# The value stage of the expert mixer: straight code, a third set of weight buffers, a third PSUM tile, weighing in quarters

## The chip, the cores and the metric

The kernel runs on one core of a Trainium2 chip. The metric is the device time of one execution in microseconds (us). Five engines work side by side: PE (TensorE, matmuls), DVE (VectorE), ACT (ScalarE), POOL (GpSimd) and SP, which only starts DMA transfers here. Each follows its own list of instructions in order; semaphores tie the lists together.

## What is computed

One inference step of a decoder layer for 512 prompt tokens and 8 sample tokens, 520 columns of width 2048, in float32: attention and a state-space layer side by side, an output projection, and then an expert mixer (PEER). The change lies in the last part of the mixer and in nothing else. The mixer picks 16 of 16384 experts per head and token:

```python
idx = jnp.take_along_axis(cand_i, top_p, axis=-1)
gate = jax.nn.softmax(top_s, axis=-1)
u = u_tab[idx]
act = jax.nn.gelu(jnp.einsum('thkd,td->thk', u, hb).astype(jnp.float32))
v = v_tab[idx].astype(jnp.float32)
return jnp.einsum('thk,thkd->td', gate * act, v).astype(h.dtype)
```

After it come the residual addition and a final norm.

## The kernel before

The 520 columns are split by how the experts are applied. For 360 of them (`ND`) the kernel computes all experts densely: the stage before (`stage_e`) multiplies the token matrix with all of `u_tab` and stores the activations and the gates in DRAM (`expert_acts`, `expert_gates`); the value stage, `stage_f`, multiplies gate x activation with all of `v_tab`. For the other 160 columns it fetches the chosen rows with indirect DMAs and sums them up: 128 steps of one row of 2048 numbers for each of 128 tokens (`vg`, 1 MB a step), and 128 steps of a quarter row for the other 32 tokens (`vgx`, 0.25 MB).

**Units.** `v_tab` comes as 128 units of 1 MB (`units`), a unit being 16 weight tiles of 128x128. A matmul in float32 is made of three matmuls on parts: weights and activations are each split into a rounded high part (`wh`, `vh`) and a rest (`wl`, `vl`), and `wh*vh + wh*vl + wl*vh` is summed in PSUM (lines 1940 to 1942). So a unit takes 2 output tiles (`VT`) x 8 expert blocks (`GRP`) x 3 = 48 matmuls of 360 columns. Eight units (`UPG`) make a group, which works on one set of 8 activation blocks; there are 16 groups (`NG`).

**The way of a unit.** SP asks for it (`load_unit`, line 116) when POOL has finished the low part of the unit two before it, whose raw buffer it takes. ACT casts the high part in two instructions (`split_hi`, line 122) once the raw data are there and PE has finished the unit two before (`tile_done`), whose buffers `wh` and `wl` it takes. POOL subtracts the low part in four instructions of 128x512 (`split_lo`, line 129); PE then multiplies. There are two sets of `raw`, `wh`, `wl`, by the parity of the unit.

**What else is in the lists.** POOL issues behind the low part of a unit 9/8 gathers of each kind on average (lines 1872 and 1877). DVE adds each finished output tile from PSUM to `x` (line 2025, 128x360), behind a unit's first tile it adds gathered rows (line 1984), behind its second the quarter rows (line 1991). PE may begin a tile when DVE has added the tile two before it (`sum_added`); there is one PSUM bank for each of a unit's two tiles. For the next group DVE multiplies activations by gates (`weigh`, line 1970), ACT casts the result to `vh` (`w_hi`, line 1885), DVE subtracts `vl` (`low`, line 1974), each in two halves of 128x1440, at the unit numbers 3, 4 and 5 of a group. SP's list also has the loads of the next activations (line 1839, 1.44 MB, behind unit request 1 of a group, when PE has begun the group) and gates (line 1843, 1.44 MB, behind unit request 5).

**Loops.** PE, ACT and SP run two groups per turn of a hardware loop, seven turns, and the last two groups as straight code. POOL and DVE have straight code throughout. The order in each list is the order of the code; no scheduler changes it.

The three lines that follow set when PE may start a unit and a tile:

```python
pe.wait_ge(m.lo_done, u + 3)
for d in range(VT):
    pe.wait_ge(S["sum_added"], i * (2 * UPG * VT) + (UPG * VT * gg + VT * n + d + 1))
```

Of the kernel before, what the change touches and what calls it, by code (L numbers as in the profile page):

```python
# [8 lines left out]
F32 = mybir.dt.float32  # L9
F32R = mybir.dt.float32r  # L10
# [5 lines left out]
ds = bass.ds  # L16
# [1314 lines left out]
UPG, VT = 8, 2  # L1331
GW = 4
# [461 lines left out]
def rows_by(j):  # L1794
    return min(HK, j * 9 // 8)
# [4 lines left out]
def rows_x_by(j):  # L1800
    return min(HK, max(0, (j - 1) * 9 // 8))

def stage_f(nc, m, ins, outs):
# [6 lines left out]
    y_sb = at("y_sb", [P, D]); yx_sb = at("yx_sb", [P, DX])  # L1810
    sq = at("sq3", [P, 4, T]); rs = at("rs3", [P, T])
    vgx = [at(f"vgx{j}", [P, DX]) for j in range(GX)]
# [5 lines left out]
    S = {n: sem("g_" + n) for n in "ain1 weighed weighed_hi weighed_lo sum_added tile_done rows_added y_kept y_turned squares_ready squares_added squares_summed root_ready out_ready out_stored x_added x_turned".split()}  # L1818
# [3 lines left out]
    halves = [slice(GRP // 2 * h, GRP // 2 * (h + 1)) for h in range(2)]  # L1822
    with nc.Block() as block:
        def turn_loads(sp, i, last):
            for gg in range(2):
                g = i * 2 + gg
# [327 lines left out]
```

## Time and profile before

| | |
|---|---|
| median of 3 runs | 3609.88 us (3597.08 to 3615.14) |
| profiled execution, its own time | 3603.36 us |
| its span | 3601.5 us |
| PE busy | 3347.8 us, 93% |
| POOL busy | 2335.4 us, 65% |
| DVE busy | 2195.3 us, 61% |
| ACT busy | 1105.8 us, 31% |
| DMA | 970.60 MB, mean 269 GB/s |

The profile is of one execution. Busy time counts the instructions of an engine; PE's matmuls overlap, so that each shows twice the time from one start to the next. "Idle before" an instruction is put down to what released it last. "Issue" is idle time in which an engine waited for nothing that the profile shows. The granted clock of PE is given as a share of 2.4 GHz. Times within the program are counted from the start of the span.

### The profile page before, as it was taken

What the parts mean: (1) busy time and instruction counts of PE and PEld (TensorE: products, weight loads), DVE (VectorE), ACT (ScalarE), POOL (GpSimd) and SP (SyncE); (2) the same over time, 40 slices, a digit from 0 to 9 for tenths busy, and PEclk for the clock granted to TensorE, in tenths of its full rate; (3) what the DMA queues carried; (4) which work ended last, traced back from release to release, by engine and by line L of the source; (5) the groups of instructions that cost most, each with busy time, mean ns of one, the idle gap of its engine ahead of it and who ended that gap; (6) DMA issues with size and microseconds to landing.
All of it is one profiled execution on the core that took longest, in us unless ns stands there. A gap on an engine that the chain in (4) does not pass through costs nothing. (4 is left out here: it accounts for less than half of the span.)

```text
span 3601.5 us, 58870 instructions
## 1 busy us (share of the span) xinstructions
PE 3347.8 (93%) x22639; PEld 3154.7 (88%) x22639; DVE 2195.3 (61%) x3999; ACT 1105.8 (31%) x1501; POOL 2335.4 (65%) x1923
## 2 busy tenths in 40 slices
PE   7999987889999999999999999988899899998997
PEld 7988853548998998999999999988898899898987
DVE  7832223335226999996887666444667566666654
ACT  4111132243223233444444344322222222222222
POOL 2533306003442458888888888877888888888874
PEclk9999988999999999999999999999999999999998
DMA  4597978672322235888888889878888888888863
GB/s 163 190 370 308 339 282 274 228 250 106 127 97 95 82 116 209 322 344 331 334 333 343 340 325 350 340 268 322 322 320 326 333 319 316 329 313 323 325 250 118
DMA packets 251675, 970.60 MB, mean 269 GB/s; under 512 B 44674, under 2 KB 108803, under 8 KB 172931
## 3 DMA queue, kind: packets, MB, share of 16 engines
q1 hardware_dynamic: 151394, 553.25, 42.6%
q0 software_dynamic: 57344, 335.58, 23.1%
q10 hardware_dynamic: 42720, 78.87, 6.0%
q8 instruction: 137, 2.24, 0.3%
q14 instruction: 80, 0.65, 0.0%
HBM read 891.32 MB, written 73.92 MB: 268 GB/s over the span
## 5 line engine op out<-in xcount | busy, mean ns | idle before, releaser
L129 POOL TENSOR_TENSOR wl<-raw,wh 128x512 fp32r<-128x512 f32 x1280 | 1712.6, 1371 | 791.7 <-ACT wh L122 789.3
L122 ACT ACTIVATE wh<-raw 128x1024 fp32r<-128x1024 f32 x648 | 650.6, 1052 | 2038.7 <-PE acc L1942 658.5
L1940 PE MATMUL acc<-vh,wh 128*128 128x360 f32 x2048 | 687.9, 336 | 107.1 <-DVE xt L2025 35.6
L1560 PE MATMUL acc<-hh,wh 128*128 128x360 f32 x2048 | 677.7, 331 | 8.0 <-POOL wl L129 8.0
L1942 PE MATMUL acc<-vh,wl 128*128 128x360 f32 x2048 | 683.0, 333 | 0.0
L1941 PE MATMUL acc<-vl,wh 128*128 128x360 f32 x2048 | 681.9, 333 | 0.0
L1562 PE MATMUL acc<-hh,wl 128*128 128x360 f32 x2048 | 671.3, 328 | 0.0
L1561 PE MATMUL acc<-hl,wh 128*128 128x360 f32 x2048 | 671.0, 328 | 0.0
L147 PE MATMUL acc<-hh,wh 128*128 128x256 f32 (+1 forms) x1920 | 547.7, 285 | 7.8 <-DVE tt L427 5.1
L148 PE MATMUL acc<-hl,wh 128*128 128x256 f32 (+1 forms) x1920 | 544.6, 284 | 0.0
L149 PE MATMUL acc<-hh,wl 128*128 128x256 f32 (+1 forms) x1920 | 543.2, 283 | 0.0
L1940 PEld LDWEIGHTS acc<-vh,wh 128*128 128x128 f32 x2048 | 395.9, 193 | 108.2 <-issue 49.8
L1941 PEld LDWEIGHTS acc<-vl,wh 128*128 128x128 f32 x2048 | 395.9, 193 | 16.4 <-issue 16.4
L1722 DVE SCALAR_TENSOR_TENSOR ug<-ug,aux 128x2048 f32<-128x2048 f32 x128 | 291.7, 2282 | 189.2 <-DMA ug<-expert_u,idx 188.4
L1984 DVE SCALAR_TENSOR_TENSOR aux<-vg,w,aux 128x2048 f32<-128x2048 f32 x127 | 298.8, 2353 | 175.4 <-DMA vg<-expert_v,idx 174.4
L1942 PEld LDWEIGHTS acc<-vh,wl 128*128 128x128 f32 x2048 | 395.4, 193 | 0.0
L1560 PEld LDWEIGHTS acc<-hh,wh 128*128 128x128 f32 x2048 | 384.6, 188 | 10.5 <-issue 10.5
L147 PEld LDWEIGHTS acc<-hh,wh 128*128 128x128 f32 x1920 | 364.2, 190 | 24.1 <-issue 24.0
L1561 PEld LDWEIGHTS acc<-hl,wh 128*128 128x128 f32 x2048 | 385.2, 188 | 0.0
L1562 PEld LDWEIGHTS acc<-hh,wl 128*128 128x128 f32 x2048 | 385.0, 188 | 0.0
L148 PEld LDWEIGHTS acc<-hl,wh 128*128 128x128 f32 x1920 | 363.9, 190 | 0.1
L149 PEld LDWEIGHTS acc<-hh,wl 128*128 128x128 f32 x1920 | 363.6, 189 | 0.0
(361 smaller groups left out, 4163.1 us busy)
## 6 DMA issues: line engine op xcount, KB each, us to landing
raw<-units SPq DMA_DIRECT2D x324, 1024.0 KB, 4.9
kr<-cache_k SPq DMA_DIRECT2D x128, 512.0 KB, 6.6
vr<-cache_v SPq DMA_DIRECT2D x128, 512.0 KB, 6.0
expert_acts<-ast ACTq DMA_DIRECT2D x128, 180.0 KB
expert_gates<-gs ACTq DMA_DIRECT2D x15, 1536.0 KB, 7.2
a<-expert_acts SPq DMA_DIRECT2D x16, 1440.0 KB, 11.1
g<-expert_gates SPq DMA_DIRECT2D x16, 1440.0 KB, 10.9
output_steps<-qo ACTq DMA_DIRECT2D x16, 288.0 KB, 6.6
```

The source lines that it names most:

```text
L122: act.activation(m.wh[s][:, k:k + KT // 2, :], m.raw[s][:, k:k + KT // 2, :], ACT.Copy).then_inc(m.hi_done, 1)
L129: x = pool.tensor_tensor(m.wl[s][:, part, :], m.raw[s][:, part, :], m.wh[s][:, part, :].bitcast(F32), ALU.subtract)
L147: pe.matmul(o, m.wh[s][:, k, :], rhs_hi[:, k, c0:c0 + n], start=(k == k_range[0]), stop=False)
L148: pe.matmul(o, m.wh[s][:, k, :], rhs_lo[:, k, c0:c0 + n], start=False, stop=False)
L149: mm = pe.matmul(o, m.wl[s][:, k, :], rhs_hi[:, k, c0:c0 + n], start=False, stop=(k == k_range[-1]))
L1560: pe.matmul(o, m.wh[s][:, k, :], m.hh[:, k, N0:T], start=(k == 0), stop=False)
L1561: pe.matmul(o, m.wh[s][:, k, :], m.hl[:, k, N0:T], start=False, stop=False)
L1562: mm = pe.matmul(o, m.wl[s][:, k, :], m.hh[:, k, N0:T], start=False, stop=(k == KT - 1))
L1940: pe.matmul(o, m.wh[s][:, VT * e + d, :], vh[gg][:, e, :], start=(e == 0), stop=False)
L1941: pe.matmul(o, m.wh[s][:, VT * e + d, :], vl[gg][:, e, :], start=False, stop=False)
L1942: mm = pe.matmul(o, m.wl[s][:, VT * e + d, :], vh[gg][:, e, :], start=False, stop=(e == GRP - 1))
L1984: dve.scalar_tensor_tensor(y_tok, vg[k % GW][:, :], m.w0[:, k:k + 1], y_tok, ALU.mult, ALU.add).then_inc(S["rows_added"], 1)
```

## The change

- `stage_f` has no loops: PE, ACT and SP get straight code.
- `raw`, `wh`, `wl` come in three sets (`RW`); unit v uses set v mod 3. SP asks for unit v when the low part of unit v-3 is done, and ACT casts it when PE has finished unit v-3.
- Output tiles go to three PSUM banks in turn (`AW`), so that PE may begin a tile when the tile three before has been added.
- `weigh`, `w_hi` and `low` work on four quarters of 128x720 (`NQ`), `weigh` behind the second tile of units 2 to 5 of a group, `low` behind that of units 3 to 6.
- The gates are loaded behind unit request 1 of a group (2 in the first), the activations behind request 4. At the start the raw request of unit 2 goes ahead of the gates.
- POOL's gathers stand one unit later in its list. Scratch buffers move to make room.

```diff
@@ -1329,6 +1329,7 @@
 NEG = -3.0e38
 GRP, NG = 8, 16
 UPG, VT = 8, 2
+RW, AW, NQ = 3, 3, 4
 GW = 4
...
 def rows_by(j):
-    return min(HK, j * 9 // 8)
+    return min(HK, max(0, (j - 1) * 9 // 8))
...
 def rows_x_by(j):
-    return min(HK, max(0, (j - 1) * 9 // 8))
+    return min(HK, max(0, (j - 2) * 9 // 8))
...
     vh = [at(f"vh{s}", [P, GRP, ND], F32R) for s in range(2)]
-    y_sb = at("y_sb", [P, D]); yx_sb = at("yx_sb", [P, DX])
...
+    raw, wh, wl = (x + [at(n, [P, KT, P], dt)] for x, n, dt in ((m.raw, "raw2", F32), (m.wh, "wh2", F32R), (m.wl, "wl2", F32R)))
+    vgx = [at(f"vgx{j}", [P, DX]) for j in range(GX - 1)]
     assert m.end <= m.x0 + 3 * KT * T * 4
...
+    vgx.append(at(f"vgx{GX - 1}", [P, DX]))
+    sq = at("sq3", [P, 4, T], off=m.first_off); rs = at("rs3", [P, T], off=m.first_off + 4 * T * 4)
+    y_sb = at("y_sb", [P, D], off=m.first_off + GRP * ND * 4); yx_sb = at("yx_sb", [P, DX], off=m.first_off + GRP * ND * 4 + D * 4)
+    tile_acc = (m.acc[:, 0, 0, 0:ND], m.acc[:, 0, 1, 0:ND], m.acc[:, 1, 1, 0:ND])
...
+    raw_in = m.raw_in + [S["raw2_in"]]
...
+    parts = [slice(GRP // NQ * q, GRP // NQ * (q + 1)) for q in range(NQ)]
...
-        def turn_loads(sp, i, last):
...
-                    if end and n >= UPG - 2:
-                        continue
-                    load_unit(m, sp, i * (2 * UPG) + (U_EXP_V + UPG * gg + n + 2), n % 2)
-                    if n == 1 and not end:
-                        load_acts(sp, g, 1 - gg)
-                    if n == 5 and not end and not (last and gg == 0):
-                        load_gates(sp, g)
-
-        def load_acts(sp, g, s):
-            sp.wait_ge(S["tile_done"], g * (UPG * VT) + 1)
-            sp.dma_start(a4[s][:, :, :], m.aD[ds(g * GRP + GRP, GRP), :, :].rearrange("e p n -> p e n")).then_inc(ain[s], 16)
-
-        def load_gates(sp, g):
-            sp.wait_ge(S["weighed"], g * GRP + 2 * GRP)
-            sp.dma_start(m.gates[:, :, :, :].rearrange("p b e n -> p b (e n)"), m.gD[:, :, ds(g * GRP + 2 * GRP, GRP), :].rearrange("b p e n -> p b (e n)")).then_inc(m.gates_in, 16)
...
-            sp.wait_ge(S["weighed"], GRP)
-            sp.dma_start(m.gates[:, :, :, :].rearrange("p b e n -> p b (e n)"), m.gD[:, :, GRP:2 * GRP, :].rearrange("b p e n -> p b (e n)")).then_inc(m.gates_in, 16)
-            with sp.Fori(0, NG // 2 - 1) as i:
-                turn_loads(sp, i, False)
-            turn_loads(sp, NG // 2 - 1, True)
+            for v in range(2, N_EXP):
+                if v >= RW:
+                    sp.wait_ge(m.lo_done, U_EXP_V + v)
+                sp.dma_start(raw[v % RW][:, :, :].rearrange("p k n -> p (k n)"), m.units[U_EXP_V + v, :, :]).then_inc(raw_in[v % RW], 16)
+                g, n = v // UPG, v % UPG
+                if n == (2 if g == 0 else 1) and g + 1 < NG:
+                    sp.wait_ge(S["weighed"], GRP * g + GRP)
+                    sp.dma_start(m.gates[:, :, :, :].rearrange("p b e n -> p b (e n)"), m.gD[:, :, GRP * g + GRP:GRP * g + 2 * GRP, :].rearrange("b p e n -> p b (e n)")).then_inc(m.gates_in, 16)
+                if n == 4 and g + 1 < NG:
+                    if g > 0:
+                        sp.wait_ge(S["tile_done"], UPG * VT * g)
+                    sp.dma_start(a4[(g + 1) % 2][:, :, :], m.aD[GRP * g + GRP:GRP * g + 2 * GRP, :, :].rearrange("e p n -> p e n")).then_inc(ain[(g + 1) % 2], 16)
...
-                u = U_EXP_V + j
                 if j < N_EXP - 2:
-                    split_lo(m, pool, u + 2, u % 2)
+                    v = j + 2
+                    for k in range(0, KT, KT // 4):
+                        if k % (KT // 2) == 0:
+                            pool.wait_ge(m.hi_done, (U_EXP_V + v) * 2 + (1 + 2 * k // KT))
+                        part = slice(k, k + KT // 4)
+                        x = pool.tensor_tensor(wl[v % RW][:, part, :], raw[v % RW][:, part, :], wh[v % RW][:, part, :].bitcast(F32), ALU.subtract)
+                    x.then_inc(m.lo_done, 1)
...
-            def w_hi(g, s, h):
-                act.wait_ge(S["weighed"], g * GRP + (GRP + GRP // 2 * (h + 1)))
-                act.wait_ge(S["tile_done"], g * (UPG * VT) + 1)
-                act.activation(vh[s][:, halves[h], :], a4[s][:, halves[h], :], ACT.Copy).then_inc(S["weighed_hi"], GRP // 2)
+            def w_hi(g, q):
+                act.wait_ge(S["weighed"], GRP * g + GRP // NQ * (q + 1))
+                if g >= 2:
+                    act.wait_ge(S["tile_done"], UPG * VT * (g - 1))
+                act.activation(vh[g % 2][:, parts[q], :], a4[g % 2][:, parts[q], :], ACT.Copy).then_inc(S["weighed_hi"], GRP // NQ)
...
-                for gg in range(2):
-                    end = last and gg == 1
-                    for n in range(UPG):
-                        if not (end and n >= UPG - 2):
-                            split_hi(m, act, i * (2 * UPG) + (U_EXP_V + UPG * gg + n + 2), n % 2, i * UPG + ((U_EXP_V + UPG * gg) // 2 + n // 2 + 1),
-                                     (S["tile_done"], i * (2 * UPG * VT) + (UPG * VT * gg + VT * (n + 1))))
-                        if n in (3, 4) and not end:
-                            w_hi(i * 2 + gg, 1 - gg, n - 3)
...
-            with act.Fori(0, NG // 2 - 1) as i:
-                turn(i, False)
-            turn(NG // 2 - 1, True)
-            for k in range(KT - 2, KT):
+            for v in range(2, N_EXP):
+                act.wait_ge(raw_in[v % RW], raw_count(v))
+                if v >= RW:
+                    act.wait_ge(S["tile_done"], VT * (v - RW + 1))
+                for k in range(0, KT, KT // 2):
+                    act.activation(wh[v % RW][:, k:k + KT // 2, :], raw[v % RW][:, k:k + KT // 2, :], ACT.Copy).then_inc(m.hi_done, 1)
+                g, n = (v - 2) // UPG, (v - 2) % UPG
+                if 3 <= n < 3 + NQ and g + 1 < NG:
+                    w_hi(g + 1, n - 3)
+                if v == N_EXP - UPG:
+                    act.wait_ge(S["rows_added"], HK)
+                    act.wait_ge(S["x_added"], HK)
+                    for g in range(4):
+                        act.activation(y_sb[:, 512 * g:512 * g + 512], m.aux[:, g, :], ACT.Copy)
+                    act.activation(yx_sb[:, :], yx, ACT.Copy).then_inc(S["y_kept"], 1)
+                if v - RW >= N_EXP - UPG:
+                    for k in range(VT * (v - RW - N_EXP + UPG), VT * (v - RW - N_EXP + UPG + 1)):
...
         def _(pe):
-            def turn(i, last):
-                for gg in range(2):
-                    for n in range(UPG):
-                        u = i * (2 * UPG) + (U_EXP_V + UPG * gg + n)
-                        s = n % 2
-                        pe.wait_ge(m.lo_done, u + 3)
-                        for d in range(VT):
-                            pe.wait_ge(S["sum_added"], i * (2 * UPG * VT) + (UPG * VT * gg + VT * n + d + 1))
-                            o = m.acc[:, 0, d, 0:ND]
-                            for e in range(GRP):
-                                if n == 0 and d == 0:
-                                    pe.wait_ge(S["weighed_lo"], i * (2 * GRP) + (GRP * gg + e + 1))
-                                pe.matmul(o, m.wh[s][:, VT * e + d, :], vh[gg][:, e, :], start=(e == 0), stop=False)
-                                pe.matmul(o, m.wh[s][:, VT * e + d, :], vl[gg][:, e, :], start=False, stop=False)
-                                mm = pe.matmul(o, m.wl[s][:, VT * e + d, :], vh[gg][:, e, :], start=False, stop=(e == GRP - 1))
-                            mm.then_inc(S["tile_done"], 1)
...
-            with pe.Fori(0, NG // 2 - 1) as i:
-                turn(i, False)
-            turn(NG // 2 - 1, True)
+            for v in range(N_EXP):
+                g, n, b = v // UPG, v % UPG, v % RW
+                pe.wait_ge(m.lo_done, U_EXP_V + v + 3)
+                for d in range(VT):
+                    r = VT * v + d
+                    pe.wait_ge(S["sum_added"], r + 1)
+                    for e in range(GRP):
+                        if n == 0 and d == 0:
+                            pe.wait_ge(S["weighed_lo"], GRP * g + e + 1)
+                        pe.matmul(tile_acc[r % AW], wh[b][:, VT * e + d, :], vh[g % 2][:, e, :], start=(e == 0), stop=False)
+                        pe.matmul(tile_acc[r % AW], wh[b][:, VT * e + d, :], vl[g % 2][:, e, :], start=False, stop=False)
+                        mm = pe.matmul(tile_acc[r % AW], wl[b][:, VT * e + d, :], vh[g % 2][:, e, :], start=False, stop=(e == GRP - 1))
+                    mm.then_inc(S["tile_done"], 1)
...
-            dve.sem_inc(S["sum_added"], VT)
-            def weigh(g, h):
-                s = g % 2
-                dve.wait_ge(ain[s], (g // 2) * 16 + 16)
+            dve.sem_inc(S["sum_added"], AW)
+            def weigh(g, q):
+                dve.wait_ge(ain[g % 2], (g // 2) * 16 + 16)
                 dve.wait_ge(m.gates_in, g * 16 + 16)
-                a = a4[s][:, halves[h], :].rearrange("p e (b n) -> p e b n", b=NB)
-                dve.tensor_tensor(a, a, m.gates[:, :, halves[h], :].rearrange("p b e n -> p e b n"), ALU.mult).then_inc(S["weighed"], GRP // 2)
-            def low(g, h):
-                s = g % 2
-                dve.wait_ge(S["weighed_hi"], g * GRP + GRP // 2 * (h + 1))
-                dve.tensor_tensor(vl[s][:, halves[h], :], a4[s][:, halves[h], :], vh[s][:, halves[h], :].bitcast(F32), ALU.subtract).then_inc(S["weighed_lo"], GRP // 2)
+                a = a4[g % 2][:, parts[q], :].rearrange("p e (b n) -> p e b n", b=NB)
+                dve.tensor_tensor(a, a, m.gates[:, :, parts[q], :].rearrange("p b e n -> p e b n"), ALU.mult).then_inc(S["weighed"], GRP // NQ)
+            def low(g, q):
+                dve.wait_ge(S["weighed_hi"], GRP * g + GRP // NQ * (q + 1))
+                dve.tensor_tensor(vl[g % 2][:, parts[q], :], a4[g % 2][:, parts[q], :], vh[g % 2][:, parts[q], :].bitcast(F32), ALU.subtract).then_inc(S["weighed_lo"], GRP // NQ)
...
-                        dve.tensor_tensor(x, x, m.acc[:, 1, 1, :].rearrange("p (c q n) -> p q c n", c=4, n=NX), ALU.add)
+                        dve.tensor_tensor(x, x, m.acc[:, 1, 0, :].rearrange("p (c q n) -> p q c n", c=4, n=NX), ALU.add)
...
-                        dve.tensor_tensor(x, x, m.acc[:, 0, d, 0:ND], ALU.add).then_inc(S["sum_added"], 1)
+                        dve.tensor_tensor(x, x, tile_acc[r % AW], ALU.add).then_inc(S["sum_added"], 1)
...
-                        if d == 0 and g + 1 < NG and n in (3, 4):
-                            weigh(g + 1, n - 3)
-                        if d == 1 and g + 1 < NG and n in (4, 5):
-                            low(g + 1, n - 4)
+                        if d == 1 and g + 1 < NG and 2 <= n < 2 + NQ:
+                            weigh(g + 1, n - 2)
+                        if d == 1 and g + 1 < NG and 3 <= n < 3 + NQ:
+                            low(g + 1, n - 3)
```

Two places in the lists show it. The first is SP's queue in the loop (before) and in a later group (now); `raw_61`, `raw_62` and `raw_21629` are the raw buffers, `a` the activations and `g` the gates. Before, one half of the loop's body:

```order
L116 DMA raw_62<-units 128x2048
L1838 ISA
L1839 ISA
L1839 DMA a_21624<-expert_acts 128x8x360
L115 REGISTER_ALU
L116 ISA
L116 DMA raw_61<-units 128x2048
```

Now, from the gates to the activations of one group:

```order
L1848 DMA g_13571<-expert_gates 128x15x192
L1844 DMA raw_21629<-units 128x2048
L1844 DMA raw_61<-units 128x2048
L1844 DMA raw_62<-units 128x2048
L1852 DMA a_13570<-expert_acts 128x8x360
```

The register work is gone, the raw requests go round three buffers, and gates and activations have traded places within the group.

The second is DVE in the units in which the next group is weighed; `xt<-xt,acc` is the addition of a tile, `aux` and the second `acc` are the sums of gathered rows. Before:

```order
L2025 TENSOR_TENSOR xt<-xt,acc 128x360
L1991 SCALAR_TENSOR_TENSOR acc<-vgx_21636,wx,acc 128x512
L1974 TENSOR_TENSOR vl_21626<-a_21624,vh_21628 128x1440
L2025 TENSOR_TENSOR xt<-xt,acc 128x360
L1984 SCALAR_TENSOR_TENSOR aux<-vg_21638,w_13556,aux 128x2048
```

Now:

```order
L1980 SCALAR_TENSOR_TENSOR acc<-vgx_21632,wx,acc 128x512
L1960 TENSOR_TENSOR a_21624<-a_21624,g_13571 128x720
L1963 TENSOR_TENSOR vl_21626<-a_21624,vh_21628 128x720
L2014 TENSOR_TENSOR xt<-xt,acc 128x360
L1973 SCALAR_TENSOR_TENSOR aux<-vg_21637,w_13556,aux 128x2048
```

A piece of weighing and a piece of low part, half as long each, now stand together behind the second tile.

## Rows read from the trace of the kernel before

**Rows 1.** Stretches: value stage, stage before, 80 units; column heads first

```profile
core 0: us, PE busy (x) PEld busy (x) DVE busy (x) ACT busy (x) POOL busy (x), PEclk, DMA share, GB/s
2423.30:3577.40 1154.10, 1059.64 (x6163) 1042.39 (x6164) 719.58 (x601) 307.90 (x308) 941.13 (x760) 0.96 0.80 303
1296.80:2410.00 1113.20, 1103.60 (x6894) 1100.44 (x6893) 846.23 (x1543) 443.50 (x493) 944.87 (x768) 1.00 0.83 314
2578.36:3298.43 720.07, 661.74 (x3840) 650.37 (x3841) 473.74 (x380) 188.22 (x180) 613.70 (x500) 0.96 0.85 322
```

**Rows 2.** Timeline of PE: start us, us, engine, line, instruction [idle before <-releaser]

```profile
2822.68 0.32 PE L1940 MATMUL acc<-vh,wh 128*128 128x360 f32 x1
...
2824.00 0.32 PE L1942 MATMUL acc<-vh,wl 128*128 128x360 f32 x1
2827.39 0.43 PE L1940 MATMUL acc<-vh,wh 128*128 128x360 f32 x1 [3.07 <-POOL wl L129]
...
2829.47 0.50 PE L1941 MATMUL acc<-vl,wh 128*128 128x360 f32 x1
```

**Rows 3.** Waits of PE, value stage: us in total, times, longest

```profile
PE acc L1940 <- DVE xt L2025: 35.6, 32, 3.9
PE acc L1940 <- POOL wl L129: 31.7, 12, 10.8
PE acc L1940 <- issue: 26.7, 11, 3.0
PE acc L1940 <- DVE vl L1977: 12.7, 1, 12.7
```

**Rows 4.** Timeline of PE at a back edge of the loop

```profile
2864.75 0.43 PE L1940 MATMUL acc<-vh,wh 128*128 128x360 f32 x1 [2.27 <-issue]
...
2870.05 0.46 PE L1940 MATMUL acc<-vh,wh 128*128 128x360 f32 x1 [2.56 <-issue]
```

**Rows 5.** Groups by line, PE, 3305 to 3577.4 us, behind the last back edge

```profile
L1940 PE MATMUL acc<-vh,wh 128*128 128x360 f32 x507 | 168.8, 333 | 13.1 <-DVE xt L2025 8.6 <-POOL wl L129 4.5
```

**Rows 6.** Groups by line, POOL, the 80 units: busy us, mean ns | idle before

```profile
L129 POOL TENSOR_TENSOR wl<-raw,wh 128x512 fp32r<-128x512 f32 x320 | 417.2, 1337 | 63.6 <-ACT wh L122 62.8
L1872 POOL DMA_INDIRECT vg<-expert_v,idx x90 | 104.5, 1162 | 15.3 <-issue 12.5
L1877 POOL DMA_INDIRECT vgx<-expert_v,idxx x90 | 92.9, 1032 | 27.4 <-issue 27.4
```

**Rows 7.** Timeline of POOL and of DVE, unit 14

```profile
2560.34 5.03 POOL L129 TENSOR_TENSOR wl<-raw,wh 128x512 fp32r<-128x512 f32 x4
2565.52 2.19 POOL L1872 DMA_INDIRECT vg<-expert_v,idx  x1 [0.16 <-issue]
2568.02 0.95 POOL L1877 DMA_INDIRECT vgx<-expert_v,idxx  x1 [0.30 <-issue]
...
2561.04 5.85 DVE L1974 TENSOR_TENSOR vl<-a,vh 128x1440 fp32r<-128x1440 f32 x1
```

**Rows 8.** Timeline of SP's queue and of ACT, start of the value stage

```profile
2428.96 10.15 SPq L116 DMA_DIRECT2D raw<-units  x2
...
2446.70 2.00 ACT L122 ACTIVATE wh<-raw 128x1024 fp32r<-128x1024 f32 x2 [18.00 <-DMA raw<-units]
2449.18 2.00 ACT L122 ACTIVATE wh<-raw 128x1024 fp32r<-128x1024 f32 x2 [0.48 <-DMA raw<-units]
```

**Rows 9.** DMA: all of 2578 to 3298 us; the fastest 8 us (columns as Rows 1)

```profile
DMA packets 61453, 231.84 MB, mean 322 GB/s; under 512 B 4480, under 2 KB 33920, under 8 KB 39680
...
2812.00:2820.00 8.00, 7.79 (x47) 7.79 (x48) 4.98 (x7) 0.00 (x0) 5.55 (x5) 1.00 1.03 414
```

**Rows 10.** Timeline of PE, the larger part of the transposes of y

```profile
3512.89 1.91 PE L1950 MATMUL aux<-ident,y_sb 128*128 128x128 f32 x16
```

**Rows 11.** Groups by line, DVE, the 80 units

```profile
L1984 DVE SCALAR_TENSOR_TENSOR aux<-vg,w,aux 128x2048 f32<-128x2048 f32 x90 | 211.7, 2353 | 117.8 <-DMA vg<-expert_v,idx 116.9
L2025 DVE TENSOR_TENSOR xt<-xt,acc 128x360 f32<-128x360 f32 x160 | 83.7, 523 | 128.3 <-PE acc L1942 128.3
L1991 DVE SCALAR_TENSOR_TENSOR acc<-vgx,wx,acc 128x512 f32<-128x512 f32 x90 | 67.3, 748 | 1.0
```

More of the change, by code:

```diff
@@ L1809, in stage_f @@
     vh = [at(f"vh{s}", [P, GRP, ND], F32R) for s in range(2)]
-    y_sb = at("y_sb", [P, D]); yx_sb = at("yx_sb", [P, DX])
-    sq = at("sq3", [P, 4, T]); rs = at("rs3", [P, T])
-    vgx = [at(f"vgx{j}", [P, DX]) for j in range(GX)]
+    raw, wh, wl = (x + [at(n, [P, KT, P], dt)] for x, n, dt in ((m.raw, "raw2", F32), (m.wh, "wh2", F32R), (m.wl, "wl2", F32R)))
+    vgx = [at(f"vgx{j}", [P, DX]) for j in range(GX - 1)]
     assert m.end <= m.x0 + 3 * KT * T * 4
@@ L1821, in stage_f, with raw_count @@
     vgx_in = [sem(f"g_vgxin{j}") for j in range(GX)]
[L1822 removed]
+    parts = [slice(GRP // NQ * q, GRP // NQ * (q + 1)) for q in range(NQ)]
+    def raw_count(v):
+        return 16 * ((U_EXP_V // 2 + 1 if v % RW < 2 else 1) + v // RW)
     with nc.Block() as block:
[L1824 to L1843 removed]
         def load_tiles(eng, n):
@@ L1895, in square @@
                     act.wait_ge(S["squares_added"], k - 3)
-                act.wait_ge(S["sum_added"], VT + UPG * VT * (NG - 1) + k + 1)
+                act.wait_ge(S["sum_added"], AW + UPG * VT * (NG - 1) + k + 1)
                 act.activation(sq[:, k % 4, :], m.xt[:, k, :], ACT.Square).then_inc(S["squares_ready"], 1)
-            def turn(i, last):
-                for gg in range(2):
-                    end = last and gg == 1
-                    for n in range(UPG):
-                        if not (end and n >= UPG - 2):
-                            split_hi(m, act, i * (2 * UPG) + (U_EXP_V + UPG * gg + n + 2), n % 2, i * UPG + ((U_EXP_V + UPG * gg) // 2 + n // 2 + 1),
-                                     (S["tile_done"], i * (2 * UPG * VT) + (UPG * VT * gg + VT * (n + 1))))
-                        if n in (3, 4) and not end:
-                            w_hi(i * 2 + gg, 1 - gg, n - 3)
-                        if last and gg == 0 and n == UPG - 2:
-                            act.wait_ge(S["rows_added"], HK)
-                            for g in range(4):
-                                act.activation(y_sb[:, 512 * g:512 * g + 512], m.aux[:, g, :], ACT.Copy)
-                            act.wait_ge(S["x_added"], HK)
-                            act.activation(yx_sb[:, :], yx, ACT.Copy).then_inc(S["y_kept"], 1)
-                        if end and n >= 1:
-                            for k in range(VT * n - 2, VT * n):
-                                square(k)
@@ L1921, in _ @@
+            for k in range(VT * (UPG - RW), KT):
                 square(k)
@@ L1954, in _ @@
-            with pe.Fori(0, NG // 2 - 1) as i:
-                turn(i, False)
-            turn(NG // 2 - 1, True)
+            for v in range(N_EXP):
[11 more added lines that the diff above has]
+                    mm.then_inc(S["tile_done"], 1)
+                if v == N_EXP - UPG - 1:
+                    pe.wait_ge(S["y_kept"], 1)
+                    for c in range(4):
+                        mm = pe.transpose(m.acc[:, 1, 0, P * c:P * c + P], yx_sb[:, P * c:P * c + P], m.ident[:, :])
+                    mm.then_inc(S["x_turned"], 1)
+                    for k in range(KT):
+                        mm = pe.transpose(m.aux[:, k // 4, P * (k % 4):P * (k % 4) + P], y_sb[:, P * k:P * k + P], m.ident[:, :])
+                        if k % 4 == 3:
+                            mm.then_inc(S["y_turned"], 1)
```

15 lines of the change are left out of this document (2 added, 13 removed).

## The prediction

> **What bounds the kernel now.** I read the stretch view first. The value stage runs from 2423.3 to 3577.4 us, 1154.1 us, with PE busy 92% and its clock at 0.96. The stage before it, with as many weight units and some 730 small matmuls more, keeps PE busy 99% at clock 1.00 in 1113.2 us [rows 1]. So the value stage loses what its twin doesn't. The floor: eight starts between 2822.68 and 2824.00 are 0.165 us apart [rows 2]; a unit has 48 matmuls, 7.91 us, and 128 units take 1012.5 us. The stage is 141.6 us above that. The waits of PE name 35.6 us for DVE's tile additions, 31.7 us for POOL's low parts, 26.7 us as "issue", and 12.7 us at the first low activations [rows 3]: 106.7 us. The other 35 us are the clock: after an idle time of 3.07 us the matmuls soon show 0.50 us instead of 0.33 [rows 2], the 1.2 GHz level instead of 2.4; it lasts for 12 of them, whose starts are 0.30 us apart. Clock loss follows long idle times, and goes when they go.
>
> "Issue" has a place. It is where the loop of 16 units branches back: PE stops 2.27 us there and 2.56 us eleven matmuls later [rows 4], at each of the six back edges. After the last back edge, over 32 units of which the last 16 are straight code, PE never waits on issue [rows 5].
>
> The other two waits come from an engine that PE hardly shows. POOL per unit, over 80 units in the loop (720.07 us, 9.00 us each): 417.2 + 104.5 + 92.9 us busy, and 12.5 + 27.4 us of issue gaps between its DMA requests [rows 6]. That is 654.5 us, **8.18 us a unit, more than PE's 7.91**. POOL is idle only 62.8 us [rows 6], because with two sets of buffers it can't begin a unit's low part before PE has left the set: it may never work ahead, and it never makes up for a late raw unit.
>
> **The change, part by part.**
>
> *Loops out on PE, SP, ACT.* Removed: six back edges, each 4.8 us idle and some 12 slow matmuls of 0.135 us extra, 6.5 us, so 39 us. They aren't a gain of their own: behind them POOL is late next, so they count only down to POOL's pace, below. Added: 5376 matmuls of code to fetch. Straight code showed no issue wait in rows 5, so zero; the ends are zero and one stop of 2.27 us plus slow clock at any interval (a rival).
>
> *Three sets of weight buffers.* A raw unit was asked for when the low part two units earlier ended, now three earlier. POOL needs it 2 x 9.00 - 5.03 - 1.05 = 11.9 us later before, and about 3 x 8.35 - 6.1 = 19 us later now (5.03 us is one burst of four low-part subtractions [rows 7], 1.05 us a half of the cast, 2.00 us [rows 8]). The slowest landing took from 2428.96 to 2446.70, 17.7 us [rows 8]. So a late raw unit is covered, and cast and low part of a unit can start a unit earlier. POOL can now work without idling: this is the part that pays. SP's queue: the gates request now waits for the last quarter of weighing and holds back the raw requests behind it by a few us; the 19 us cover it. If that cover were gone, the raw unit would be late as before, about 3 us of PE every two groups [rows 2].
>
> *Tiles in three PSUM banks.* DVE may be one tile (3.95 us) later before PE waits. That hides most of the 35.6 us. What is late next is POOL.
>
> *Weighing in quarters.* DVE's low part of 1440 elements, begun at 2561.04 inside a burst of POOL's, took 5.85 us and ended 1.5 us after the burst [rows 7]: 1.5 us is its work, the rest a wait for the memory port that both use. In turn POOL's request at 2565.52 took 2.19 us instead of 0.95, while DVE held the port. Free of each other, POOL needs 5.03 + 1.125 x 2 x 0.95 + 39.9/80 = 7.67 us a unit (1.125 is 90 requests of each kind on 80 units). Eight pieces of 720 elements, 0.85 us each (on the line from 0.52 us for 360 elements [rows 11] to 1.5 us for 1440), are 6.8 us a group, 0.85 a unit, and a POOL that never idles can lose all of it. Bounds of POOL's need: 8.18 (as measured, with idle time in which to hide) and 7.67 + 0.85 = 8.52. I take 8.35, between the two, because POOL's idle share, which hid part of it, goes.
>
> The Trainium skill (SBUF — State Buffer, the section on the shared port pair) says that the loser of that port blocks until the winner's instruction ends. Rows 7 differ: DVE waited past the ends of all four of POOL's subtractions. By the page DVE would wait 1.26 us at most, its tiles would never be late, and POOL would lose the port at every piece: 8.52 us a unit, and the sum would be 19 us higher.
>
> *Gathers one unit later in POOL's list.* POOL itself is a unit earlier, so they go out at the same time in PE's terms. Nothing.
>
> *The start.* Raw unit 2 was asked for at 2428.96, behind gates and x tiles, and cast at 2446.70, with PE idle 10.8 us [rows 3, 8]. Now it goes first, about 2422, and units 3 and 4 take its old places: casts at 2446.7 and 2449.2. PE wants unit 3 at 2449.7 and gets it at 2453: 3 us. Unit 5 comes behind the 1.44 MB of activations, 2.5 MB more at some 375 GB/s, an estimate from the loop's 322 GB/s on average and 414 GB/s in the fastest 8 us [rows 9], 6.6 us: POOL starts its low part at 2457 and from there has no reason to idle.
>
> *The sum.* Low part of unit 115, the last one before which gathers stand, ends at 2457 + 110 x 8.35 + 5.03 = 3380.5. Then 13 units of PE, 102.8 us, and the transposes, 2 us [rows 10], and 1 us of waits: PE ends at 3486 instead of 3577.4. Saved: 91.5 us. The end of the program behind it (norm and stores) is as before. The profiled execution took 3603.4 us, so 3512; the median of the runs is 6.5 us above it, so **3518 us** as a median, 2.5% less.
>
> **Rivals.**
>
> *PE becomes the bound* (POOL loses nothing to the port and keeps 7.67). For it: in the stage before PE was 99% busy with the same POOL work. Against: there a unit took 8.7 us because of the extra matmuls. Then PE ends at 2423.3 + 1012.5 + 1.6 (one spell of slow clock) + 3 + 2 = 3442.4, 135 us saved: 3475.
>
> *DVE holds the tiles back: slower.* Product and low part now stand together behind the second tile of five units in eight. DVE's unit: 2 x 0.52 + 1.125 x (2.35 + 0.75) + 2 x 0.85 = 6.2 us [rows 11], and 11.3 us if it waits out one burst of 5.03 us each time, 16.3 if POOL takes the port between the two. PE runs ahead of it by only three tiles. At 11.3 us for five units it falls 14.8 us behind the 8.35, and with the one tile of 3.95 us that it may be later PE would stop 11 us a group, 165 us over 15 groups: 3683. It decides from 91/75 = 1.2 us a unit on. For it: PE does wait for DVE's additions now [rows 3]. Against: having waited for a burst's end, DVE is next back one POOL period later, in the same gap of POOL's, so it is as slow as POOL and no slower. A mild form, a quarter to a third of that, gives 3560 to 3573.
>
> *DMA is the bound.* The loop moved 231.84 MB in 720 us, 2.90 MB a unit, at a busy share of 0.85 [rows 1, 9]; 8.35 us a unit asks for 347 GB/s and a share of 0.92. For it: 0.92 leaves little room. Against: 414 GB/s was reached for 8 us, at a share of 1.03 [rows 9], and this is 19% above what is asked for. If 322 GB/s were the ceiling, the loop would stay at 9.0 us a unit and only start and end gain: 3590, no change.
>
> *Code fetch stalls straight code: slower.* 2.3 to 3 us idle and the slow clock, some 4.6 us a stop; from 20 stops, one in 6 units, it eats the gain. Against: rows 5.
>
> **How the numbers follow.** POOL's pace 0.70 (3490 to 3550), PE's 0.10 (3475), DVE in its mild form 0.08, in its strong one 0.04, DMA 0.05, code fetch 0.03 (half of it slower). A run of this kernel tells 0.5%, 18 us, from no change. Faster by more: 0.70 + 0.10 + 0.08 + a third of the DMA case, 0.90; within: 0.04; slower: 0.06. The range, 3474 to 3562, takes in PE's pace below, POOL at 8.52 us (3537) and the beginning of the mild DVE case above.
>
> **What would show it.** No issue waits on PE in the value stage; ACT's casts waiting for raw data only at the start; POOL idle by under 2% between 2457 and the last gather, with 8.2 to 8.6 us a unit; clock 0.99; PE's remaining waits under 1 us each, on the low parts or on tile additions. Wrong if POOL still waits for casts and PE for DVE's additions by over 1 us in the weighing units (DVE), if raw landings of over 19 us appear (DMA), or if "issue" is back (code).

## The result and the profile after

Four runs of the changed kernel gave a median of **3572.66 us** (3566.12 to 3575.93); the kernel before, beside it, 3607.48 us (4 runs). The ratio is 0.9893, 95% interval 0.9867 to 0.9918: faster by 1.1%. The forecast was 3518 us, 2.5% less, with a range from 3474 to 3562. The direction was right; the size was not, and the time lies outside the range. The profiled execution took 3571.98 us, its span is 3570.2 us.

Windows of the changed kernel; the columns are those of [rows 1], and the first stretch is the value stage:

```profile
2419.40:3547.30 1127.90, 1048.89 (x6164) 1043.42 (x6164) 790.31 (x666) 312.20 (x340) 923.93 (x760) 0.96 0.81 310
```

The stage takes 1127.9 us and ends at 3547.3, where 3486 was forecast. The clock is still 0.96, so long stops of PE are still there. The waits of PE in this stage, to be held against [rows 3]:

```profile
PE acc L1935 <- DVE xt L2014: 69.4, 14, 6.4
PE acc L1935 <- DVE vl L1966: 12.8, 1, 12.8
PE acc L1935 <- POOL wl L1867: 7.0, 2, 5.6
```

The issue waits are gone, and POOL's 31.7 us have become 7.0. But the wait for the tile additions has doubled, from 35.6 to 69.4 us, and the number of times fell from 32 to 14: fewer and longer stops, each followed by slow matmuls. They come once a group, and from the second group on at the same place, before the fourth of its eight units. The other engines' waits in the stage:

```profile
ACT wh L1905 <- DMA raw<-units: 274.5, 40, 13.2
DVE aux L1973 <- DMA vg<-expert_v,idx: 245.8, 64, 9.6
...
POOL wl L1867 <- ACT wh L1905: 128.7, 32, 15.1
```

So POOL isn't the engine that never idles, as was forecast: it waits for ACT's casts for 128.7 us. Raw data come late, and so do gathered rows. One group of the timeline shows how the three belong together. SP's queue first, then POOL, ACT, DVE and PE (columns as in [rows 2]):

```profile
2857.59 32.96 SPq L1844 DMA_DIRECT2D raw<-units  x5
2906.81 0.38 SPq L1848 DMA_DIRECT2D g<-expert_gates  x1
2907.23 7.06 SPq L1844 DMA_DIRECT2D raw<-units  x3
2914.44 0.43 SPq L1852 DMA_DIRECT2D a<-expert_acts  x1
...
2893.06 5.03 POOL L1867 TENSOR_TENSOR wl<-raw,wh 128x512 fp32r<-128x512 f32 x4
2898.25 1.45 POOL L1872 DMA_INDIRECT vg<-expert_v,idx  x1 [0.16 <-issue]
...
2900.98 5.03 POOL L1867 TENSOR_TENSOR wl<-raw,wh 128x512 fp32r<-128x512 f32 x4
...
2914.09 1.45 POOL L1872 DMA_INDIRECT vg<-expert_v,idx  x1 [0.16 <-issue]
...
2922.62 5.05 POOL L1867 TENSOR_TENSOR wl<-raw,wh 128x512 fp32r<-128x512 f32 x4 [5.83 <-ACT wh L1905]
2927.81 0.96 POOL L1872 DMA_INDIRECT vg<-expert_v,idx  x1
...
2921.48 2.01 ACT L1905 ACTIVATE wh<-raw 128x1024 fp32r<-128x1024 f32 x2 [11.92 <-DMA raw<-units]
...
2903.41 3.37 DVE L1960 TENSOR_TENSOR a<-a,g 128x720 f32<-128x720 f32 x1
...
2937.71 4.81 DVE L1973 SCALAR_TENSOR_TENSOR aux<-vg,w,aux 128x2048 f32<-128x2048 f32 x2 [9.24 <-DMA vg<-expert_v,idx]
2942.44 0.52 DVE L2014 TENSOR_TENSOR xt<-xt,acc 128x360 f32<-128x360 f32 x1
...
2943.11 0.64 PE L1935 MATMUL acc<-vh,wh 128*128 128x360 f32 x1 [5.07 <-DVE xt L2014]
2943.54 0.50 PE L1936 MATMUL acc<-vl,wh 128*128 128x360 f32 x1
```

Read it from the top. POOL's low part ends at 2898.09 and frees a raw buffer, but SP stands at the gates request, which waits for the last product piece; that piece ends at 2906.78. The raw request goes at 2907.23, 9.1 us late, and ACT casts that unit from 2921.48 on, 23.4 us after its buffer came free. While SP stands there the DMA engines run dry, and then they get gates (1.44 MB), three raw units in 7 us and the activations (1.44 MB) at once. The hold is 9.1 or 9.2 us at all 14 gates requests behind the first. In the kernel before no raw request goes over 1 us after its buffer came free: there the gates are asked for behind unit 7 of a group, counted as in the change by the unit asked for, and weighing is over before the next buffer comes free. Windows of the same group:

```profile
2903.36:2908.36 5.00, 5.00 (x32) 5.00 (x32) 5.00 (x5) 1.50 (x2) 4.54 (x5) 1.00 0.23 75
2918.36:2923.36 5.00, 5.00 (x32) 5.00 (x32) 1.25 (x3) 1.88 (x2) 0.74 (x1) 1.00 1.02 424
2938.36:2943.36 5.00, 0.26 (x1) 0.29 (x2) 4.89 (x4) 1.78 (x2) 4.67 (x5) 0.82 1.03 424
```

The share falls to 0.23 and then is 1.00 or more for some 35 us. ACT waits 11.92 us for raw data and POOL 5.83 us for ACT. The gathers stand behind that low part in POOL's list, so the next one goes 13.7 us after the last one (2914.09 to 2927.81) instead of 7.9, and into full DMA engines. DVE waits 9.24 us for its row, with the tile additions behind it in its list, and PE runs out of its three tiles and stops for 5.07 us.

### The profile page after: what moved, and what is told of

The parts are those of the page before. It is cut to its first block and busy times, and to the rows that moved or that the text cites. A ratio compares the mean times of both kernels' runs of the same rounds, so it can differ in the third digit from the quotient of the medians.

```text
span 3570.2 us, 58151 instructions
## 1 busy us (share of the span) xinstructions
PE 3331.6 (93%) x22639; PEld 3149.4 (88%) x22639; DVE 2276.9 (64%) x4059; ACT 1109.2 (31%) x1531; POOL 2319.5 (65%) x1923
## 5 line engine op out<-in xcount | busy, mean ns | idle before, releaser
L1935 PE MATMUL acc<-vh,wh 128*128 128x360 f32 x2048 | 683.9, 334 | 89.4 <-DVE xt L2014 69.4
L1867 POOL TENSOR_TENSOR wl<-raw,wh 128x512 fp32r<-128x512 f32 x504 | 649.8, 1324 | 130.7 <-ACT wh L1905 128.7
L1562 PEld LDWEIGHTS acc<-hl,wh 128*128 128x128 f32 x2048 | 385.0, 188 | 0.0
L1563 PEld LDWEIGHTS acc<-hh,wl 128*128 128x128 f32 x2048 | 384.9, 188 | 0.0
## 6 DMA issues: line engine op xcount, KB each, us to landing
a<-expert_acts SPq DMA_DIRECT2D x16, 1440.0 KB, 18.4
g<-expert_gates SPq DMA_DIRECT2D x16, 1440.0 KB, 11.2
```

The costliest lines, as they stand in the source:

```text
L1562: pe.matmul(o, m.wh[s][:, k, :], m.hl[:, k, N0:T], start=False, stop=False)
L1563: mm = pe.matmul(o, m.wl[s][:, k, :], m.hh[:, k, N0:T], start=False, stop=(k == KT - 1))
L1867: x = pool.tensor_tensor(wl[v % RW][:, part, :], raw[v % RW][:, part, :], wh[v % RW][:, part, :].bitcast(F32), ALU.subtract)
L1935: pe.matmul(tile_acc[r % AW], wh[b][:, VT * e + d, :], vh[g % 2][:, e, :], start=(e == 0), stop=False)
```

## The experiments

All times are medians. The ratio is to the kernel before, run beside each on the same chip; "early" means gathers as in the kernel before. Edits are to the changed kernel unless another is named. e1 to e4 ran on one chip, e5 to e8 on a second, e9 to e11 on a third and e12 on a fourth, and the kernel before took 3610.8, 3621.0, 3612.8 and 3617.8 us beside them. Between these sets the ratios are to be compared; a difference of times can be off by some 10 us.

| run | us | ratio, 95% interval |
|---|---|---|
| e1, gates request later | 3494.18 | 0.9668 [0.9638, 0.9697] |
| e2, gathers early | 3484.73 | 0.9648 [0.9621, 0.9675] |
| e3, small gates request | 3506.34 | 0.9708 [0.9679, 0.9738] |
| e4, before, loops written out | 3599.57 | 0.9965 [0.9945, 0.9985] |
| e5, e1 and e2 | 3506.72 | 0.9680 [0.9659, 0.9701] |
| e6, before, gathers late | 3969.21 | 1.0964 [1.0940, 1.0989] |
| e7, e2, two sets of weight buffers | 3532.25 | 0.9752 [0.9733, 0.9770] |
| e8, e2, two tile banks | 3490.25 | 0.9649 [0.9630, 0.9667] |
| e9, e2, weighing in halves | 3512.25 | 0.9721 [0.9701, 0.9742] |
| e10, e2, two banks and halves | 3514.03 | 0.9721 [0.9701, 0.9742] |
| e11, e2, first gates request later | 3487.60 | 0.9658 [0.9637, 0.9680] |
| e12, e10 with two sets of weight buffers | 3562.28 | 0.9843 [0.9792, 0.9894] |

### The chain through SP's list and POOL's list

**e1: the gates request two raw requests later in a group.**

```diff
-                if n == (2 if g == 0 else 1) and g + 1 < NG:
+                if n == (2 if g == 0 else 3) and g + 1 < NG:
```

> The changed kernel, with the gates request behind raw request 3 of a group instead of 1. Theory Q (SP's queue): the gates request waits for the last quarter of weighing and holds two raw requests back by about 8 us; then gates, three raw units and activations are on the queue at once, POOL is starved of raw data, the gathers behind its low part come late, and DVE waits for a gathered row ahead of its tile additions, which stops PE 5 us once a group. With the request moved, SP does not wait; the stop shrinks below 2 us and 15 groups give back 4 to 7 us each: 3470 to 3515. Theory D (DMA is at its ceiling whatever the order): within 5 us of 3570. Theory P (the port pieces of DVE): unchanged as well, with the stops where they are.

**e2: the gathers back where they were in POOL's list.**

```diff
 def rows_by(j):
-    return min(HK, max(0, (j - 1) * 9 // 8))
+    return min(HK, j * 9 // 8)
 def rows_x_by(j):
-    return min(HK, max(0, (j - 2) * 9 // 8))
+    return min(HK, max(0, (j - 1) * 9 // 8))
```

> The changed kernel, with the gathers in POOL's list where they stood before (one unit earlier). Theory Q: the raw data are as late as in the changed kernel and POOL waits as long, but the rows that DVE wants were requested ahead of the starved low part; the waits of DVE for rows (245.8 us) fall below 120 and PE's stops to under 2 us: 3480 to 3520. Theory D: the same bytes arrive in the same time, 3565 to 3575. Theory P: no change.

Either edit alone is enough: 78 us less than the changed kernel for e1, 88 us for e2. In e1 the gathers are as late in POOL's list as in the change, but no raw request behind the gates is late any more. The waits of PE in e1:

```profile
PE acc L1935 <- DVE xt L2014: 16.9, 10, 3.6
```

and in e2, where the tile additions are late only once:

```profile
PE acc L1935 <- POOL wl L1867: 10.2, 13, 4.1
...
PE acc L1935 <- DVE xt L2014: 1.1, 1, 1.1
```

The expectation for e2 gave the time, but not the way. It had raw data as late as in the changed kernel, POOL waiting as long, and DVE's waits for rows below 120 us; these are 160.1 us, and POOL doesn't wait between 2500 and 3200 us. The same places of SP's and POOL's lists in e2:

```profile
2868.05 0.38 SPq L1848 DMA_DIRECT2D g<-expert_gates  x1
2868.47 14.95 SPq L1844 DMA_DIRECT2D raw<-units  x3
...
2862.20 5.05 POOL L1867 TENSOR_TENSOR wl<-raw,wh 128x512 fp32r<-128x512 f32 x4
```

The low part ends at 2867.25 and the raw request goes 1.2 us later, not 9.1, in each of the 14 groups. So e2 takes away the first link as well as the last. DVE can't go on before its gather, so a gather that stands behind one low part more makes POOL stand one unit further ahead of PE: from the end of a unit's low part to PE's start on it there are 8.2 us, median of units 8 to 119, in the changed kernel, and 0.6 us in e2; it is 6.8 us in e1, with late gathers, and 0.2 in e5, with early ones. The raw buffer comes free that much earlier, while the end of weighing, for which the gates request waits, stays where PE and DVE are. Most of the 9.1 us is thus the work of the shift of the gathers itself.

ACT waits 430.5 us for raw data in e2, more than in the changed kernel, and it costs nothing while POOL is kept busy. POOL's groups in e2, 2500 to 3200 us (columns as in [rows 6]), and the windows of a stretch:

```profile
L1867 POOL TENSOR_TENSOR wl<-raw,wh 128x512 fp32r<-128x512 f32 x349 | 439.6, 1295 | 1.6
L1872 POOL DMA_INDIRECT vg<-expert_v,idx x97 | 119.6, 1233 | 16.8 <-issue 16.8
L1877 POOL DMA_INDIRECT vgx<-expert_v,idxx x99 | 93.8, 948 | 30.2 <-issue 30.2
...
2873.00:3390.00 517.00, 510.98 (x3080) 506.01 (x3079) 418.76 (x333) 154.03 (x165) 480.38 (x399) 1.00 0.92 354
```

Here is the state that the prediction described: POOL doesn't idle (1.6 us before 349 subtractions), the clock is 1.00, and the chain of waits of the whole program lies 24% on POOL. 349 subtractions are 87.25 units, so a unit takes POOL 8.02 us.

**e5: both edits together.** Its diff is those of e1 and e2.

> The changed kernel with both edits, the gates request behind raw request 3 and the gathers one unit earlier in POOL's list. Theory Q says that the two are links of one chain (SP holds raw units back, POOL starves, the gathers behind its low part are late), so that breaking it once more gives no more: the early gathers alone left 13 us over PE's floor. 3476 to 3488. If they were two separate losses, 1.5 to 2% each, it would come to 3410, which PE's floor forbids; if the later gates request harms, 3490 or more.

No gain on top. By the time it is 22 us more than e2, on another chip; the ratios, 0.9680 and 0.9648, have intervals that overlap. PE's waits for low parts have grown:

```profile
PE acc L1935 <- POOL wl L1867: 24.0, 26, 4.1
```

The gates are now asked for shortly ahead of the activations, and the two land in 12.9 and 21.6 us, median, against 11.2 and 19.9 in e2. Whether two transfers so close together are what costs time wasn't tried apart. Since e2 alone has a hold of only 1.2 us left, e5 had no second link to cut. Read from the other side it says more: against e1, with the gates request in the same late place, it puts the gathers back and gains nothing (0.9680 and 0.9668). The late gathers cost nothing that can be told once the gates request is out of the way.

**e3: the gates request fetches 1 of its 15 blocks, from the third group on.** The weighing there multiplies by stale gates.

```diff
+                    nb = NB if g < 2 else 1
-                    sp.dma_start(m.gates[:, :, :, :]
+                    sp.dma_start(m.gates[:, 0:nb, :, :]
```

> The changed kernel; from the third group on the gates request fetches 1 of its 15 blocks (0.1 MB instead of 1.44 MB), so the weights by gates are computed from stale gates, and SP's order and waits stay. 1.35 MB less a group is 3.3 us of the 410 GB/s that the burst shows. Theory D: the group gets about 3 to 4 us shorter, 13 groups, 3520 to 3530. Theory Q: the burst is shorter by 3.3 us, so raw data and rows come 3 us earlier and the stop of 5.3 us and the slow matmuls behind it shrink by 3 to 5 us a group: 3505 to 3530. Theory P: no change. It tells P from the other two.

The hold of SP is there as before (the three raw requests behind the gates still go within 7.1 us), only 1.35 of the 1.44 MB of gates are gone, and 66 us with them. PE's waits for tile additions fall to 25.7 us in 13 stops:

```profile
PE acc L1936 <- DVE xt L2015: 25.7, 13, 7.2
```

The longest of them, 7.2 us, stands in a group whose gates are still whole. So the hold alone costs a small part. The long stop needs the burst of transfers behind it.

One figure goes with all of these runs: the longest time from a raw buffer's coming free to the landing of the unit that takes it, over units 16 to 119. It is 24.7 us in the changed kernel, 18.4 in e1, 15.9 in e2, 18.7 in e3 and 20.4 in e5. The prediction had said that 19 us are covered.

**e6: the kernel before, with its gathers one unit later.** The diff is that of e2 turned round, on the kernel before.

> The kernel before, with only the gathers moved one unit later in POOL's list. The prediction held this move to cost nothing because POOL is a unit earlier; in the kernel before POOL is not. A row would be asked for 9 us later than DVE's list wants it: from a unit's end 7.4 us to the request, 8.6 to land, 2.9 for the row and the tile behind it, 18.9 us, which two banks allow only 1.5 unit times: 12.6 us a unit instead of 9.0, 3900 to 4070. If DVE's wait for rows were harmless to PE: 3600 to 3650.

The step which the prediction had priced at nothing costs 348 us where there are two tile banks and two sets of buffers. POOL can't be a unit earlier there, so this isn't the case that the prediction spoke of; it is the price without that lead. The waits of PE and of DVE:

```profile
PE acc L1940 <- DVE xt L2025: 336.0, 53, 8.7
...
DVE aux L1984 <- DMA vg<-expert_v,idx: 714.5, 116, 11.0
```

DVE waits for 116 of the 128 rows, and PE for the tile additions behind them. A stop also lasts longer than the wait says, since slow matmuls follow it: the mean clock of this program is 0.935.

### The parts of the change one by one

**e4: the kernel before with the loops of the value stage written out, on SP, ACT and PE.**

```diff
-            with pe.Fori(0, NG // 2 - 1) as i:
+            for i in range(NG // 2 - 1):
```

> The kernel before, with nothing but its loops in the value stage written out (PE, ACT, SP). The six back edges cost 4.8 us idle and 1.6 us of slow clock each, 39 us. If PE's own stops bound the stage, 3565 to 3575. If POOL's pace does (8.18 us a unit against 9.0), part of it comes back as waits on POOL and DVE: 3575 to 3595. If straight code had a fetch cost: 3610 or more, with issue waits.

The waits of PE in e4:

```profile
PE acc L1940 <- DVE xt L2025: 67.6, 32, 5.1
PE acc L1940 <- POOL wl L129: 26.9, 16, 9.5
```

The 26.7 us of issue are gone. In their place the wait for tile additions has grown from 35.6 to 67.6 us: 0.35% is left, less than the expectation gave. It fits that DVE and POOL caught up while PE stood at a back edge; this was not tried apart.

**e7, e8, e9, e10, e11 and e12** all start from e2, so that the chain above doesn't hide what a part is worth:

```diff
-RW, AW, NQ = 3, 3, 4
+RW, AW, NQ = 2, 3, 4      (e7)
+RW, AW, NQ = 3, 2, 4      (e8)
+RW, AW, NQ = 3, 3, 2      (e9)
+RW, AW, NQ = 3, 2, 2      (e10)
+RW, AW, NQ = 2, 2, 2      (e12)
-                    sp.wait_ge(m.lo_done, U_EXP_V + v)
+                    sp.wait_ge(m.lo_done, U_EXP_V + v + 3 - RW)      (e7, e12)
-                if n == (2 if g == 0 else 1) and g + 1 < NG:
+                if n == (4 if g == 0 else 1) and g + 1 < NG:      (e11)
```

> The changed kernel with the early gathers (e2) and two sets of weight buffers instead of three, the rest as in the change. A raw unit then has 2 x 7.91 - 6.1 = 9.7 us to land; in the burst behind the gates it takes 13 to 18. If the third set is the part that pays: one stop of 4 to 8 us a group and slow matmuls behind it, 3560 to 3610. If straight code, banks and quarters carry the gain: 3485 to 3500.

> The changed kernel with the early gathers (e2) and tiles in two PSUM banks instead of three. DVE's tile addition may then be 3.95 us late instead of 7.9; behind a port wait of 3.4 us and a row it is about 4 to 6. If the third bank carries a part: waits on DVE of 1 to 2 us in the weighing units, 3510 to 3560. If it does nothing: 3480 to 3490.

> e2 (the changed kernel with early gathers) with weighing in halves of 128x1440 instead of quarters. In e2 POOL never idles between 2500 and 3200 us, at 8.0 us a unit, and each piece of weighing costs it 0.50 us at its next gather request. If quarters are worth something, halves make DVE hold the port 1.65 us at a time and its tile additions 5 to 8 us late: waits on DVE of 1 to 3 us twice a group, 3500 to 3540. If only the sum of port time counts, half as many pieces cost POOL as much or less: 3475 to 3488.

> e2 with two tile banks and weighing in halves: of the change only straight code, the third set of weight buffers and the order of SP's loads stand. If the third set is what lets POOL work without idling, and banks and quarters only soften DVE's lateness: 3490 to 3530, well below the 0.9965 of straight code alone. If banks and quarters carry the gain: 3560 to 3600.

> e2, with the first gates request behind the raw requests of units 3 and 4 instead of 2, so that those go out at once. It should take away the 4.1 us that PE waits for unit 3 at the start: 2 to 5 us less than e2, 3478 to 3484. If the gates of group 1 come too late for the first weighing: 3485 to 3495.

> The change with early gathers, but with two sets of weight buffers, two tile banks and weighing in halves: what is left is straight code and the new order in SP's list. Theory: the third set is most of the gain; on top of the plain order it is worth at least what it was on top of everything (48 us, e7 against e2), and more, because two banks and halves leave PE and POOL nothing to make up with: 3565 to 3600, and PE waits for POOL's low parts over 46 us. Rival A: straight code and the order of the requests carry the gain, and the third set is worth 48 us or less here too: 3535 to 3562. Rival B: without the third set nothing is left of the gain, as in e4 (3599.57): 3600 or more.

*Third set of weight buffers:* 1.0% (the ratios of e7 and e2) and 1.2% (e12 and e10, where e12's interval is half a per cent either way), less than expected of e7. On e7's own chip e8, which has three sets and two banks, is 42 us faster. In e12 a low part is late for 23.0 us in all, not for the 46 expected, and POOL waits 35.0 us for ACT within 700 us, where its idle time before subtractions is 1.6 us in e2 and in e10. PE waits another 44.1 us for tile additions there. The two gains agree within the intervals, so none is seen to depend on banks and quarters. *Third tile bank:* nothing in the time that can be told (the ratio of e8 is that of e2, and e10 is 1.8 us above e9). It does hide waits: with two banks and early gathers PE waits for DVE 17 times, but with POOL as the limit its waits for low parts fall from 10.2 to 3.7 us.

```profile
PE acc L1935 <- DVE xt L2014: 15.1, 17, 2.6
PE acc L1935 <- POOL wl L1867: 3.7, 1, 3.7
```

*Quarters:* 27.5 us (e9 against e2), 0.7% by the ratios. The time lies where the expectation put it, but not for its reason: PE waits for DVE once, 3.3 us. The cause shows in POOL's groups in e9, over the same 700 us as e2:

```profile
L1867 POOL TENSOR_TENSOR wl<-raw,wh 128x512 fp32r<-128x512 f32 x340 | 427.8, 1293 | 1.6
L1872 POOL DMA_INDIRECT vg<-expert_v,idx x96 | 130.2, 1356 | 16.8 <-issue 16.8
```

340 subtractions are 85 units, 8.24 us each against 8.02: the gather requests take 1356 ns instead of 1233 on average. Beside a piece of 1440 elements on DVE one takes 2.20 us, median of 41; beside one of 720 it takes 1.45 us, median of 69 in e2. Over 110 units that is 23 us. *The start* (e11) is worth nothing: the stop before unit 3 is gone, and one of 4.4 us before unit 5 has come. *Straight code and the new order* with early gathers (e12) stand 1.6% below the kernel before, and straight code alone (e4) 0.35%. The rest, about 1.2%, is left to the new places of the requests in SP's list and of weighing and low parts in DVE's and ACT's, which have moved too; none was tried alone.

## Why the prediction was wrong

**Loops: right, and the caution with them too.** No issue wait of PE is left. By themselves they give 0.35% (e4), not the 39 us, since others are late next.

**Code fetch: right.** 6144 matmuls of straight code show no stop on issue.

**POOL's pace as the limit: right where nothing else starves it, 8.35 us a unit was too much.** It measured 8.02 us in e2. A gather request in a weighing unit takes 0.50 us more (1.45 us instead of 0.95), at one request each, and not the 1.24 us more of [rows 7], where the piece on DVE was twice as long. With 8.02 the sum of the prediction is 110 x 0.33 = 36 us lower, 3482 us; e2, which is the change without its shift of the gathers, took 3484.7. That this is so near is in part luck: from 2460.3 us, and not 2457, POOL took 8.05 us a unit up to unit 115 in e2, some 6.5 us more in all, and the 6.5 us added for the median were only 0.4.

**"Gathers one unit later ... Nothing": this step failed.** The reason given, that POOL is itself a unit earlier, holds only while POOL is ahead. Once a group it is not, and then a gather goes 13.7 us after the one before it, behind a low part that waits for raw data. DVE takes rows in front of tile additions, so PE pays. And the step isn't passive: by it POOL must be a unit ahead, which stretches the hold at the gates request from 1.2 to 9.1 us. e2 undoes the step and gains 88 us. It failed together with the next one: with the gates request moved, late gathers cost nothing that can be told (e1 and e5).

**"Holds back the raw requests behind it by a few us; the 19 us cover it": this step failed too.** The cover of 19 us was about right; what it had to cover wasn't. The hold is 9.1 us in every such group, the unit then takes 14.2 us to land in the group shown, and 23.3 is more than 19. The hold lets the DMA engines run dry and then asks them for everything at once, and the prediction set the hold and the slowest landing against the cover one by one, never their sum. e1, which moves the request by two places, gains 78 us, and e3, which takes the bytes away, 66 us.

The two work together, which is why either repair is enough. The price of the chain: 15 stops of 3.8 to 6.4 us with slow matmuls behind each. PE's period of a group is 70.5 us, the mean of the 13 from 2492.6 to 3408.7, and 63.3 by the floor; 15 times 7 us is 105 us. Had POOL's pace of 8.02 been the limit, a group would have taken 64.2 us.

**Third tile bank: it hides waits, and brings no time.** In e8 two banks leave 15.1 us of waits for tile additions, three 1.1 us, and the times are the same, since POOL is the limit; with late gathers three banks weren't enough.

**A reading that was off.** The 12.7 us of [rows 3] for the first low activations lie ahead of the stretch, which begins with that matmul. The waits inside it are 94.0 us, so 47.6 us and not 35 are left for the rest, of which slow matmuls make up some 38. The sum doesn't use it.

**The rivals.** "DVE holds the tiles back" named the place where PE stops, and its mild form, 3560 to 3573, holds the result; but the mechanism was another, and the number is luck. DVE was late because of rows, and not because of the port: a product piece takes 3.37 us, median, in the changed kernel and in e2 alike, and in e2 no wait of PE follows from it. The Trainium skill (SBUF — State Buffer, Summary: rules for kernel authors) has the second of the two to issue wait until the first finishes. The trace differs again: the product piece begun at 2903.41 ended at 2906.78, 0.77 us behind the end of all of POOL's burst (2900.98 to 2906.01), although two of the four subtractions of 1.3 us ended in between. As in [rows 7], DVE waited out the burst, and so the port does have one share in the chain: the piece on which the gates request waits is some 2.5 us late, an estimate from its 3.37 us and the 0.85 us of work of the prediction. "DMA is the bound" is wrong as a ceiling: e2 moves 354 GB/s at a share of 0.92 with the clock at 1.00. As a matter of what is asked for at once, it was the right place to look.

**The start: right within some 3 us.** PE waits 4.1 us for unit 3 in e2, where 3 were forecast, and e11 found nothing more to be had there.

The lowest ratio is that of e2, 0.9648, 3484.7 us; e1, e5, e8 and e11 can't be told from it by the intervals.

## What to carry to other kernels

A request that waits for a semaphore holds every request behind it in its list: price it by how long the transfers run dry, and by what is asked for at once when it goes. A buffer more lets an engine run ahead, but a step put "one unit later because the engine is one unit ahead" makes that lead a need: it is spent before the first delay comes. Where two shifts in different lists each look covered by the same slack, price them together, and try each alone.

## What the runs showed of the hardware

- DMA engines at a share above 1.00 moved 424 GB/s over 5 us; 354 to 360 GB/s over 500 to 700 us left the clock of PE at 1.00 and POOL busy throughout.
- A gather request of POOL took 0.95 us alone, 1.45 us where a quarter of weighing was on DVE, 2.20 us where it was a half, and 1356 ns on average with halves against 1233 with quarters. Smaller pieces on DVE made the requests shorter, not longer.
- In the changed kernel 206 matmuls in the value stage start 0.30 us apart instead of 0.165, behind stops of PE: some 28 us on top of the idle time.
